# New order for the opening of a sparse attention: selection bias and first query on ScalarE, two rotary tiles on GpSimd, all probabilities scaled on ScalarE

## The reference

```python
h = rms_norm(x, mix_norm[l])
(a_val, a_gate, b_gate, c_gate, b_h, q, k, v, q_idx, k_idx, w_idx) = jnp.split(h @ w_in[l], SPLIT_POINTS, axis=-1)
y_a = silu(layer_norm(causal_dwconv(a_val * sigmoid(a_gate), conf_dw[l]) + conf_dw_b[l], ...))   # 31 taps, 256 channels
y_b = b_gate * causal_dwconv(c_gate * b_h, sc_dw[l])                                             # 3 taps, 256 channels
q, k, q_idx, k_idx = rope(q), rope(k), rope(q_idx), rope(k_idx)                                  # 8 heads of 64; 4 index heads
score = sum_h w_idx * relu(q_idx @ k_idx.T), causal;  keep the 128 best keys of each query
y_c = softmax(q @ k.T / 8 over the keys kept) @ v
x = x + concatenate([y_a, y_b, y_c]) @ w_out[l]
```

## Time and profile before

| | us |
|---|---|
| median of three runs (lowest, highest) | 3585.2 (3582.82, 3587.37) |
| the profiled execution's own time | 3583.34 |
| its span, first to last instruction | 3581.1 |
| PE busy in it | 3481.2 (97%) |
| mean granted TensorE clock (1 is full) | 0.991 |

### The profile page before, as it was taken

One profiled execution on the slowest core, in us unless ns is written; L12 is line 12 of the kernel. 1 busy time (PEld: TensorE's weight loads), 2 busy tenths in 40 slices (PEclk: granted clock), 3 DMA queues, 4 the chain that ended last, 5 costly groups with the idle time before them and its releaser, 6 DMA issues.

```text
span 3581.1 us, 44364 instructions
## 1 busy us (share of the span) xinstructions
PE 3481.2 (97%) x16768; PEld 2865.9 (80%) x16768; DVE 1922.2 (54%) x2934; ACT 989.1 (28%) x1714; POOL 2023.3 (56%) x1223
## 2 busy tenths in 40 slices
PE   8999998999999999998899999999999999999998
PEld 7888876888888888876788888877788887778887
DVE  5553697735541454179764553167666416666631
ACT  2120246232110111035623211035422104532210
POOL 6666564446666666666444666632366663246664
PEclk9999999999999999999899999999999999999999
DMA  4233471322233323347042223354123335312232
GB/s 143 96 96 93 116 187 42 131 70 94 97 94 99 98 96 97 98 125 179 28 138 69 97 94 96 98 144 114 49 93 99 95 103 148 101 59 94 94 95 88
DMA packets 106684, 362.43 MB, mean 101 GB/s; under 512 B 14304, under 2 KB 14720, under 8 KB 105856
## 3 DMA queue, kind: packets, MB, share of 16 engines
q1 hardware_dynamic: 91648, 319.41, 28.1%
q0 software_dynamic: 8640, 31.46, 4.7%
q10 hardware_dynamic: 6208, 8.92, 1.0%
HBM read 317.27 MB, written 2.10 MB: 89 GB/s over the span
## 4 chain that ended last, share of the span: by engine, by line
PE 82%; DVE 7%; issue 3%; ACT 3%; DMA 3%; POOL 2%; ACTq 0%; DVEq 0%; SPq 0%; POOLq 0%
PE banks L569 27%; PE banks L571 26%; PE banks L570 26%; DMA w_raw<-mid 1%; DMA w_lo<-w_raw 1%; DVE h_lo L932 1%; PE banks L994 1%; DMA qk_swap<-qk_raw 1%; DVE w_lo L610 1%; POOL bias L1375 0%; POOL w_hi L605 0%; PE banks L812 0%; DVE square_sum L693 0%; POOL bias L1378 0%; ACT w_hi L617 0%
## 5 line engine op out<-in xcount | busy, mean ns | idle before, releaser
L610 POOL TENSOR_TENSOR w_lo<-w_raw,w_hi 128x1024 fp32r<-128x1024 f32 (+1 forms) x508 | 1244.2, 2449 | 40.7
L605 POOL CAST w_hi<-w_raw 128x1024 fp32r<-128x1024 f32 (+1 forms) x540 | 564.5, 1045 | 1204.1 <-PE banks L571 1116.0
L569 PE MATMUL banks<-h_hi,w_hi 128*128 128x512 f32 x2928 | 1153.8, 394 | 28.8 <-DVE h_lo L932 13.0
L570 PE MATMUL banks<-h_lo,w_hi 128*128 128x512 f32 x2928 | 1142.5, 390 | 0.0
L571 PE MATMUL banks<-h_hi,w_lo 128*128 128x512 f32 x2928 | 1142.4, 390 | 0.0
L569 PEld LDWEIGHTS banks<-h_hi,w_hi 128*128 128x128 f32 x2928 | 551.0, 188 | 156.2 <-issue 24.3
L571 PEld LDWEIGHTS banks<-h_hi,w_lo 128*128 128x128 f32 x2928 | 551.1, 188 | 116.7
L570 PEld LDWEIGHTS banks<-h_lo,w_hi 128*128 128x128 f32 x2928 | 551.3, 188 | 110.1
L569 PE MATMUL banks<-act_hi,w_hi 128*128 128x512 f32 x1056 | 411.1, 389 | 0.9 <-DVE x L973 0.9
L570 PE MATMUL banks<-act_lo,w_hi 128*128 128x512 f32 x1056 | 410.8, 389 | 0.0
L571 PE MATMUL banks<-act_hi,w_lo 128*128 128x512 f32 x1056 | 410.8, 389 | 0.0
(11 more groups left out here) (434 smaller groups left out, 4432.8 us busy)
## 6 DMA issues: line engine op xcount, KB each, us to landing
w_raw<-gu SPq DMA_DIRECT2D x176, 512.0 KB, 3.5
w_raw<-mid SPq DMA_DIRECT2D x120, 512.0 KB, 3.5
w_raw<-up SPq DMA_DIRECT2D x88, 512.0 KB, 3.5
w_raw<-dn SPq DMA_DIRECT2D x96, 448.0 KB, 3.3
w_raw<-mix SPq DMA_DIRECT2D x62, 512.0 KB, 3.5
...
```

Of the source, the lines that this page charges most:

```text
L569: pe.matmul(out, w_hi, m_hi, start=start, stop=False, skip_group_check=True)
L570: pe.matmul(out, w_hi, m_lo, start=False, stop=False, skip_group_check=True)
L605: g.tensor_copy(wh[:, ch.slot, 0:width], raw_tile(ch, width)).then_inc(Ring.hi[ch.slot], 1)
L610: eng.tensor_tensor(wl[:, ch.slot, 0:width], raw_tile(ch, width), f32(wh[:, ch.slot, 0:width]), ALU.subtract).then_inc(Ring.split[ch.slot], 1)
```

## The change

In the first stack, per layer:
- `chosen` goes from POOL to ACT (a copy and three Relu with a new one-element bias tile `lift`), behind the eviction of projection 18.
- Head 0's query goes from POOL to ACT, between the splits of chunks 24 and 25. Head 1's query stays on POOL, and waits for the v products instead of the variance matmul.
- v's low halves: one before the attention's loop, three at its steps 1, 3 and 5, in the order `V_ORDER`; PE now waits for all of them at head 0's outputs rather than at item 2's scores.
- The convolution's norm: deviation and squares at step 2, variance matmul at 3 (was 2), Ln and Exp at 4 (was 3), refinement at 6 (was 5), scaling and Silu at 7 (was 5). ACT loads a table that has both Ln and Exp before the loop. The low halves of the short convolution move from before the loop to steps 8 and 9.
- The split of chunk 27 on ACT moves from before the loop to step 6.
- ACT scales the probabilities of all 32 items.
- Rotary tiles 9 and 10 go from DVE to POOL, behind the queries of heads 2 and 3 and behind that of head 4; DVE's tiles 7 and 8 stay at steps 2 to 11.
- The first w_out products begin at item 10 (was 8) and come a little closer together.

In the second stack: the two products of `U_CHUNK` wait for eight and nine evictions, one after the other; the L2128 matmuls stand behind product i = 3; DVE's `u_low(2)` precedes a root.

```diff
     def part_at(d):
-        return 8 + 7 * d // 2
+        return 10 + 22 * d // 7
@@ PE, scores(h, t) and outputs(h)
-            if h % 2 == 0 and t == 0 and h < 4:
-                pe.wait_ge(prope.sem, prope(l, 10 * (h // 2 + 1)))
+            if h == 4 and t == 0:
+                pe.wait_ge(rope1.sem, rope1(l, 25))
             elif h % 2 == 0 and t == 0:
-                pe.wait_ge(rope1.sem, rope1(l, 15 + 10 * (h // 2 - 1)))
+                pe.wait_ge(prope.sem, prope(l, (10, 20, None, 30)[h // 2]))
             if h == 0 and t == 2:
-                pe.wait_ge(v_lo_s.sem, v_lo_s(l, T))
+                pe.wait_ge(v_lo_s.sem, v_lo_s(l, 1))
@@
+            if h == 0:
+                pe.wait_ge(v_lo_s.sem, v_lo_s(l, T))
@@ POOL, pool_rope and q_padded
+            if n >= 7:
+                g.wait_ge(ln_y.sem, ln_y(l, 2))
@@
         elif h == 1:
-            g.wait_ge(ln_var.sem, ln_var(l, 1))
+            products_done(g, mid_chunk(l, V_CHUNK + 3))
@@
-    PADDED_AT = {V_CHUNK + 3: (0, 1), OUT_CHUNK + 2: (1, 5), OUT_CHUNK + 3: (5, 6), OUT_CHUNK + 4: (6, HEADS)}
+    PADDED_AT = {V_CHUNK + 3: (1, 2), OUT_CHUNK + 1: (2, 4), OUT_CHUNK + 2: (4, 5), OUT_CHUNK + 3: (5, 6), OUT_CHUNK + 4: (6, HEADS)}
+    V_ORDER = (2, 0, 1, 3)
+    ROPE_AT = {s: 1 for s in range(2, 12)}
@@
-    def chosen(g, l):
-        g.tensor_copy(dsa_bias(0), causal[:, 3 * P:S]).then_inc(bias_s.sem, 1)
-        g.wait_ge(topk.sem, topk(l, 3 * 2 * ROUNDS))
-        for t in range(1, T):
-            g.tensor_scalar(dsa_bias(t), dsa_bias(t), TAKEN_BELOW, -MASKED, ALU.is_gt, ALU.mult).then_inc(bias_s.sem, 1)
@@
+        if m in (OUT_CHUNK + 1, OUT_CHUNK + 2):
+            for i in range(5):
+                pool_rope(g, l, m - OUT_CHUNK + 8, i)
@@ ACT
+        def chosen():
+            act.activation(dsa_bias(0), causal[:, 3 * P:S], ACT.Copy).then_inc(bias_s.sem, 1)
+            act.wait_ge(topk.sem, topk(l, 3 * 2 * ROUNDS))
+            for t in range(1, T):
+                act.activation(dsa_bias(t), dsa_bias(t), ACT.Relu, bias=lift[:, 0:1], scale=-MASKED / -TAKEN_BELOW)\
+                    .then_inc(bias_s.sem, 1)
@@
-        for m in range(V_CHUNK + 3, OUT_CHUNK + 2):
+        own_split(V_CHUNK + 3)
+        act.wait_ge(prope.sem, prope(l, 10))
+        act.wait_ge(short_s.sem, short_s(l, 11))
+        for tile, full in ((qz_hi, qk_hi), (qz_lo, qk_lo)):
+            act.activation(tile[0][:, :], f32(full[:, 4, :]), ACT.Copy, scale=halfcol[:, 0:1]).then_inc(qz_first_s.sem, 1)
+        for m in range(OUT_CHUNK, OUT_CHUNK + 2):
             own_split(m)
@@
-        own_split(OUT_CHUNK + 2)
+        act.preload_act_table_set("natural_log_exp_and_others")
@@
-        attention_act(act, dsa, l, None, causal_tiles, pt_hi, out_hi, conv_norm, 8)
+        attention_act(act, dsa, l, None, causal_tiles, pt_hi, out_hi, conv_norm)
@@ DVE
+        value_low(0)
@@
+            if s == 1:
+                value_low(1)
+            elif s == 2:
+                v.wait_ge(ln_mean.sem, ln_mean(l, 1))
...
+            elif s in (3, 5):
+                value_low(2 + (s - 3) // 2)
+            elif s in (8, 9):
+                yab_low(s - 8, s - 6)
@@ second stack, PE
-        pe.wait_ge(zr_ev.sem, zr_ev(l, 9))
@@
         for i in (4, 5):
+            pe.wait_ge(zr_ev.sem, zr_ev(l, 4 + i))
@@
-            if i == 2:
+            if i == 3:
                 pe.wait_ge(branch_y.sem, branch_y(l, 2 * MH))
```

More of the change, by code:

```diff
@@ L196, in program @@
     one = place("one", [4])
+    lift = place("lift", [1])
     gate_cells = place("gate_cells", [8])
@@ L251, in program @@
     widx_row = acc[:, 0, :]
-    dev = place("conv_dev", [2, S], at=hh_at + 4 * S * 4)
-    dev_sq = place("conv_dev_sq", [2, S], at=hh_at + 6 * S * 4)
+    dev = place("conv_dev", [2, S], at=hh_at + 5 * S * 4)
+    dev_sq = place("conv_dev_sq", [2, S], at=hl_at)
     ln_tmp = place("conv_norm", [3, S], at=hl_at + 5 * S * 4)
+    late_rt = place("late_rope", [2, S], at=hl_at + 6 * S * 4)
     rbuf = place("relu", [2, S], at=bgate_at)
@@ L1590, in mix1_act @@
                 short_taps(1)
-        for m in range(V_CHUNK + 3, OUT_CHUNK + 2):
+            elif j == 18:
+                chosen()
+        own_split(V_CHUNK + 3)
[4 more added lines that the diff above has]
+        for m in range(OUT_CHUNK, OUT_CHUNK + 2):
             own_split(m)
         products_done(act, mid_chunk(l, V_CHUNK + 3))
-        for t in range(T):
+        for t in V_ORDER:
             act.activation(v_hi[:, t, :], bank[4 + t][:, :], ACT.Copy, scale=st[:, 2, t:t + 1]).then_inc(v_hi_s.sem, 1)
@@ L1598, in mix1_act @@
             act.activation(hh[:, 2 + k, :], yb[:, k, :], ACT.Copy).then_inc(yab_hi.sem, 1)
-        own_split(OUT_CHUNK + 2)
-        for k in range(2):
-            act.wait_ge(ln_dev.sem, ln_dev(l, k + 1))
-            act.activation(dev_sq[:, k, :], dev[:, k, :], ACT.Square).then_inc(ln_sq.sem, 1)
+        act.preload_act_table_set("natural_log_exp_and_others")
         def conv_norm(s):
-            if s == 3:
+            if s == 2:
+                for k in range(2):
+                    act.wait_ge(ln_dev.sem, ln_dev(l, k + 1))
+                    act.activation(dev_sq[:, k, :], dev[:, k, :], ACT.Square).then_inc(ln_sq.sem, 1)
+            elif s == 4:
                 act.wait_ge(ln_inv.sem, ln_inv(l, 1))
@@ L1771, in mix1_dve, with value_low @@
         v.wait_ge(conv1.sem, conv1(l, 2 * CONVW + 2))
-        for t in range(T):
-            v.wait_ge(v_hi_s.sem, v_hi_s(l, t + 1))
+        def value_low(i):
+            t = V_ORDER[i]
+            v.wait_ge(v_hi_s.sem, v_hi_s(l, i + 1))
             v.scalar_tensor_tensor(v_lo[:, t, :], bank[4 + t][:, :], st[:, 2, t:t + 1], f32(v_hi[:, t, :]),
                                    ALU.mult, ALU.subtract).then_inc(v_lo_s.sem, 1)
-        v.wait_ge(ln_mean.sem, ln_mean(l, 1))
-        for k in range(2):
-            v.scalar_tensor_tensor(dev[:, k, :], bank[2][:, :], -1.0 / 256, acc[:, k, :], ALU.mult, ALU.add)\
-                .then_inc(ln_dev.sem, 1)
+        value_low(0)
         def yab_low(i, k):
@@ L1785, in yab_low @@
                 .then_inc(yab_lo.sem, 1)
-        for i, k in enumerate((2, 3)):
-            yab_low(i, k)
         def conv_norm(s):
-            if s == 3:
+            if s == 1:
+                value_low(1)
+            elif s == 2:
+                v.wait_ge(ln_mean.sem, ln_mean(l, 1))
+                for k in range(2):
+                    v.scalar_tensor_tensor(dev[:, k, :], bank[2][:, :], -1.0 / 256, acc[:, k, :], ALU.mult, ALU.add)\
+                        .then_inc(ln_dev.sem, 1)
+            elif s in (3, 5):
+                value_low(2 + (s - 3) // 2)
+            elif s in (8, 9):
+                yab_low(s - 8, s - 6)
+            if s == 4:
                 v.wait_ge(ln_var.sem, ln_var(l, 1))
@@ L1825, in rope_in @@
         def rope_in(s):
-            n, i = divmod(s - 2, 5)
-            if 0 <= n < 4:
-                rope_step(7 + n, i)
-        attention_dve(v, dsa, l, SCORE_BANKS, dsa_bias, causal_tiles, pt_hi, pt_lo, out_lo, ahead_of, rope_in, 8)
+            for step in range(sum(ROPE_AT.get(e, 0) for e in range(s)), sum(ROPE_AT.get(e, 0) for e in range(s + 1))):
+                rope_step(7 + step // 5, step % 5)
+        attention_dve(v, dsa, l, SCORE_BANKS, dsa_bias, causal_tiles, pt_hi, pt_lo, out_lo, ahead_of, rope_in)
     def xat_dve(v, l):
```

52 lines of the change are left out of this document (29 added, 23 removed).

## The result

The changed kernel takes 3567.24 us (median of 4 runs, 3565.99 to 3567.82), before takes 3586.28 (4 runs, 3582.82 to 3591.66). The profiled executions differ by 15.1 us of span (3581.1 to 3566.0). The rest lies in what was not profiled: before's profiled execution was at the fast end of its runs, the changed one's (3567.82) at the slow end of its own.

The account below looks back on a forecast made before the run. PE was taken as the bound, busy 3481.2 of 3581.1 us, with the opening on DVE's and ACT's chain. Two layers' 3.0 plus the second stack's 4.0 gave 3576.3 profiled, median 3578.2 us, range 3570 to 3589.

Parts of the forecast that it names:

- the later waits: Behind item 11, PE's waits grow by an estimated 1.5 us a layer, including head 5's query coming 0.7 late.
- head 1's query beside the convolution: Its pair on POOL waits only for v's products, so it runs during the convolution and costs that 1.9 us.
- the second stack: PE's waits for the gates' eviction and `probs` go: 4.5 us in all, 4.0 taken for a possibly late eighth eviction.
- this buys nothing by itself: Before v's products: chunk 24 arriving 7.9 us earlier removes PE's 3.73 us wait, but the mean still waits for DVE's convolution.
- The convolution's end: DVE's last sum ahead of the mean in layer 1 comes 0.6 us earlier, at 535.1.
- The opening: From the convolution's end to item 11's scores takes 27.3 us, putting these at 562.4, 6.0 earlier than before.
- The clock: PE idles some 5 us before the mean, so mean and variance may run at half clock: 1.5 us lost a layer.
- worth nothing there: Behind item 11 DVE was not the bound, so taking two rotary tiles and eight scalings off it gains nothing.
- the hidden rival: DVE's new order takes back ACT's savings and second-stack waits reappear at the next product: 3585 us, chance 0.08.
- The lock: Rival: POOL's operations beside DVE's opening each hold DVE up 0.97 us, 2.0 more a layer: 3582.2 us, chance 0.12.
- The slower one: Rival: late rotary tiles on POOL take 2.65 us an operation beside DVE, delaying head 5's query: 3588 to 3596, chance 0.10.
- The larger gain: Rival: head 1's pair misses the convolution and the clock stays up, 4.5 us a layer: 3572.2 us, chance 0.20.

Follow-up runs that it names:

- e1: The kernel before with only the selection bias moved from POOL to ACT behind projection 18: median 3581.7 us, ratio to before 0.9992.
- e4: The changed kernel with the selection bias back on POOL, in front of chunk 24's transfer: median 3575.7 us, ratio to before 0.9966.
- e8: The changed kernel with rotary tiles 9 and 10 back on DVE: median 3569.0 us, ratio to before 0.9949.
- e2: The kernel before with only the second stack's edits: median 3584.1 us, ratio to before 0.9990.
- e3: The changed kernel with the second stack's edits undone: median 3569.9 us, ratio to before 0.9955.
- e9: The changed kernel with the selection bias and head 0's query both back on POOL: median 3574.7 us, ratio to before 0.9967.

## Why the prediction was wrong

It had the place of the gain (the opening's chain) and mis-sized three terms and one condition. The terms are the later waits (1.5 lost forecast, 1.5 gained in layer 1), head 1's query beside the convolution (1.9 forecast, 0.4 measured) and the second stack; the condition is "this buys nothing by itself", said of chunk 24's transfer. For each layer 1.5 was forecast, and 6.0 and 7.8 were measured.

- **Chunk 24's transfer.** The wait went as forecast; v's products ended at 530.1 (529.3 forecast). "This buys nothing by itself" is left open by e1 in the old order: layer 1 gained 1.6 us there, the ratio says 2.9 with an interval that includes nothing, and the faster six runs lie 7 below before. In the new order it failed: e4 is 8.4 slower (6.8 against its own before), because v's halves then head the chain.
- **The convolution's end.** Forecast 535.1, measured 533.7. The step that failed is "head 1's pair now falls into the convolution" at 1.9 us. The pair cost it 0.4; POOL did the waiting, 3.68 and 5.09 us.
- **The opening.** Forecast 27.3 from the convolution's end to item 11, measured 28.9 (533.77 to 562.67), 1.8 of it the mean at the lower clock. With the earlier start, item 11 came at 562.67, forecast 562.4: two errors that cancel, which is luck. The forecast's path also ended elsewhere: it ran over exp 8 and the transposes, while PE's last wait ahead of item 11 was 2.38 us for DVE's low halves, held up by tile 9 on POOL (e8).
- **The clock.** The 1.5 us deducted for it were right in size for layer 1: 1.8 in the mean's row, which is already in the 28.9. In layer 2 the mean took 3.20 and the variance 3.09. But before loses by the clock as well, as below.
- **Given back.** The two w_out products are as forecast (four before item 11 before, two after). "Later waits: 1.5" has the wrong sign: PE's idle time behind item 11 fell from 3.5 to 2.0 us. Head 5's query was not late: it was ready at 581.94 and wanted at 582.33, since tile 10 took 5.9 us (569.43 to 575.37) in place of 6.4, and the operations around it some 0.9 less. e8, with the tiles back, has 1.5 and 2.2 us more behind item 11: "worth nothing there" is the step that failed.
- **Layer 2** gave 7.8, by the same steps: beside the 6.0 that it starts earlier, item 11 comes 6.3 earlier (1722.64 to 1710.31), and PE's idle time behind it fell from 3.8 to 1.2 us. The clock has a part in it. Each kernel has stretches near the lower level with PE at work, before and, behind the dots, the changed kernel some 13 us earlier:

```profile
1715.00:1720.00 5.00, 5.00 (x20) 4.27 (x20) 2.77 (x9) 1.46 (x6) 0.00 (x0) 0.56 0.00 0
...
1700.00:1705.00 5.00, 4.91 (x23) 4.30 (x21) 5.00 (x10) 4.95 (x10) 4.77 (x4) 0.65 0.00 0
1705.00:1710.00 5.00, 3.08 (x8) 2.42 (x9) 4.79 (x15) 4.99 (x13) 1.48 (x2) 0.70 0.55 105
```

  PE's busy time times the missing share of the clock, summed over such stretches, is an estimate of the cost. In layer 2 it gives 7.9 us before (6.0 of them from 1700 to 1720) and 6.0 changed; in layer 1 it gives 3.1 before and 4.5 changed. So by this estimate layer 1 lost 1.4 us by the clock and layer 2 got 1.9 back, which the prediction did not consider.

- **Second stack.** 4.0 forecast, 1.3 in the profiles, 0 to 4 by e2 and e3; the wait for `qn_lo` took the place of the others, as the hidden rival had it for this part.
- **The rivals.** The lock exists on both sides. Beside the convolution GpSimd waited for VectorE more than it held it up. In tile 9 it held VectorE up: six 512-column operations from 553.28 on took 7.3 us together in place of 4.0 in e8 (four of them are in e8's rows above), most of it hidden behind ACT. The slower one did not occur: tile 9's operations took 0.95 to 1.72, not 2.65. Its counter-argument was misread, though: beside the tile of the earlier trace rows VectorE was at the top-k until 482.79, and the convolution had only begun. The larger gain was the nearest, and right on the convolution (533.7 beside 533.1), but wrong on the clock; by its own terms (1.5 + 1.5 + 2.0) it is 5.0 a layer, not 4.5. The slower one's "3.7 us of loss a layer" leaves out the second stack's 4.0; with it, it is 5.6.
- **The sum.** Layer 1 for one: 1.5 forecast, plus 1.4 (convolution), plus 3.0 (later waits), is 5.9, beside 6.0; that it fits so well is in part luck, as the opening's 1.6 more and the clock's 1.5 cancel. The remaining 4 us between the profiles' 15.1 and the medians' 19 lie in executions without a profile. That before's slower runs have a long POOL wait, as e1's has, is not shown, and the profiles speak against it for the query: in all six layers of before, e2 and e9 it took 2.6. Only the bias copy varies there (7.1 to 8.4).

By the Trainium skill (SBUF — State Buffer, SBUF: two separate sides) of a VectorE operation with two SBUF inputs and a GpSimd operation, the one that starts first gets the shared pair for its whole instruction and the other fully blocks. The rows agree that each holds the other up (in before, five multiply-adds took 5.25 us in place of 3.3 beside head 0's two operations, which took 4.2 in place of 3.1); whether for the whole instruction they do not settle. They add that a run of VectorE operations can keep GpSimd out for many instructions, 16.90 us in e1.
